# Who issues the reload of the residual: the sync engine among its weight slots, or ScalarE ahead of its casts

## What is computed

```
x   = x   + gate   * (concat(branches, latent)  @ w_out[l])
ctx = ctx + gate_c * (concat(branches, context) @ w_out[l])    # layers 0 and 2 only
```

## Time and profile before

| | us |
|---|---|
| median of 3 runs (3209.92 to 3211.33) | 3210.18 |
| the profiled execution | 3207.1 |
| its span | 3205.3 |
| TensorE busy in it | 3001.5 (94%) |
| VectorE, ScalarE busy | 1604.0, 1023.6 |
| mean granted TensorE clock | 0.969 of full |

### The profile page before, as it was taken

One profiled execution on the slowest core, in us unless ns is written; L12 is line 12 of the kernel. 1 busy time (PEld: TensorE's weight loads), 2 busy tenths in 40 slices (PEclk: granted clock), 3 DMA queues, 4 the chain that ended last, 5 costly groups with the idle time before them and its releaser, 6 DMA issues. The chain is left out here.

```text
span 3205.3 us, 40895 instructions
## 1 busy us (share of the span) xinstructions
PE 3001.5 (94%) x17158; PEld 2356.6 (74%) x17158; DVE 1604.0 (50%) x2493; ACT 1023.6 (32%) x1508; POOL 102.1 (3%) x157
## 2 busy tenths in 40 slices
PE   5899999999997999998969999999989979999988
PEld 1577777786775787886847779667767758797888
DVE  2334343356435553455555472555564355738574
ACT  2212233224212333433323221334442123215453
POOL 0000000000000000000000000430000000003100
PEclk7899999999998999999989999999999989999999
DMA  7644433321544544632844444323345533222455
GB/s 322 280 161 148 145 119 130 113 79 47 208 169 166 213 165 147 248 125 79 310 173 152 157 158 158 131 99 133 135 175 188 183 101 118 82 90 93 145 166 170
DMA packets 120135, 495.10 MB, mean 154 GB/s; under 512 B 11792, under 2 KB 30480, under 8 KB 95120
## 3 DMA queue, kind: packets, MB, share of 16 engines
q1 hardware_dynamic: 99648, 463.51, 40.6%
q10 hardware_dynamic: 20304, 28.97, 2.6%
HBM read 484.05 MB, written 8.39 MB: 154 GB/s over the span
## 5 line engine op out<-in xcount | busy, mean ns | idle before, releaser
L1307 PE MATMUL products<-h_high,w_high 128*128 128x512 f32 (+1 forms) x3424 | 1256.4, 367 | 89.3 <-DVE h_low L936 45.7
L1307 PE MATMUL products<-h_low,w_high 128*128 128x512 f32 (+1 forms) x3424 | 1189.6, 347 | 0.0
L1307 PE MATMUL products<-h_high,w_low 128*128 128x512 f32 (+1 forms) x3424 | 1189.3, 347 | 0.0
L853 DVE TENSOR_TENSOR w_low<-w_raw,w_high 128x1024 fp32r<-128x1024 f32 x500 | 615.3, 1231 | 817.8 <-ACT w_high L550 815.0
L550 ACT CAST w_high<-w_raw 128x1024 fp32r<-128x1024 f32 x500 | 522.8, 1046 | 1381.0 <-PE products L1307 1332.0
L1307 PEld LDWEIGHTS products<-h_high,w_high 128*128 128x128 f32 x3424 | 658.0, 192 | 340.1 <-issue 226.9
L1307 PEld LDWEIGHTS products<-h_low,w_high 128*128 128x128 f32 x3424 | 659.6, 193 | 81.0 <-issue 13.0
L1307 PEld LDWEIGHTS products<-h_high,w_low 128*128 128x128 f32 x3424 | 657.9, 192 | 81.6
L1307 PE MATMUL products<-w_high,h_high 128*128 128x256 f32 x640 | 184.1, 288 | 0.5 <-issue 0.5
L1307 PE MATMUL products<-w_high,h_low 128*128 128x256 f32 x640 | 181.1, 283 | 0.0
L1307 PE MATMUL products<-w_low,h_high 128*128 128x256 f32 x640 | 181.0, 283 | 0.0
(11 more groups left out here) (193 smaller groups left out, 2639.9 us busy)
## 6 DMA issues: line engine op xcount, KB each, us to landing
w_raw<-w_slots SPq DMA_DIRECT2D x500, 512.0 KB, 3.5
ada_w<-ada_slots SPq DMA_DIRECT2D x174, 1024.0 KB, 6.0
mix_b<-ada_slots SPq DMA_DIRECT2D x18, 1024.0 KB, 9.7
x_residual<-x ACTq DMA_DIRECT2D x2, 4096.0 KB, 23.1
x_scratch<-x_residual ACTq DMA_DIRECT2D x3, 2048.0 KB, 7.9
x_residual<-x_scratch ACTq DMA_DIRECT2D x3, 2048.0 KB, 9.2
x_residual<-ctx ACTq DMA_DIRECT2D x2, 2048.0 KB, 15.0
out<-x_residual ACTq DMA_DIRECT2D x1, 2048.0 KB, 7.8
```

What stands on the lines that cost most here:

```text
L853: nc.vector.tensor_tensor(wlo[:, n % SPL, :], raw[:, n % RAW, :], whi[:, n % SPL, :].bitcast(F32), ALU.subtract).then_inc(low_done, 1)
L1307: ins = nc.tensor.matmul(o, a, b, start=first and q == 0, stop=last and q == 2, skip_group_check=skip)
```

## The change

The reloads leave ScalarE's `ysplit`. SP issues them in the first round of `out`, ahead of s4, and waits for the ends of the phases before `ysplit` first.

```diff
+            def x_again(pi):
+
+                layer = PH[pi - 1]["layer"]
+                for s in ends.values():
+                    sp.wait_ge(s, pi - 1)
+                if layer == 0:
+                    sp.dma_start(xT[:, :, :], dram["x0"]).then_inc(x_in, 16)
+                    return
+
+                sp.wait_ge(x_out, 16 * layer)
+                sp.dma_start(xT[:, :, LAT], dram["x_scratch"]).then_inc(x_in, 16)
+                if layer < 3:
+
+                    sp.dma_start(xT[:, :, 0:S], dram["ctx2"]).then_inc(x_in, 16)
...
                         for k in range(8):
+                            if ph["name"] == "out" and i == 0 and k == 4:
+                                x_again(pi)
                             slot(n0 + 8 * i + k)
...
                     layer = ph["layer"]
-                    if layer == 0:
-                        act.dma_start(xT[:, :, :], dram["x0"]).then_inc(x_in, 16)
-                    else:
-                        act.wait_ge(x_out, 16 * layer)
-                        act.dma_start(xT[:, :, LAT], dram["x_scratch"]).then_inc(x_in, 16)
-                        if layer < 3:
-
-                            act.dma_start(xT[:, :, 0:S], dram["ctx2"]).then_inc(x_in, 16)
```

More of the change, by code:

```diff
@@ L456, in unit @@
                 sp.dma_start(place, was[u, :, :]).then_inc(landed, 16)
-            for ph in PH:
+            def x_again(pi):
[9 more added lines that the diff above has]
+                    sp.dma_start(xT[:, :, 0:S], dram["ctx2"]).then_inc(x_in, 16)
+            for pi, ph in enumerate(PH):
                 at = ph["at"]
```

## The result

| | before | after |
|---|---|---|
| median of 13 runs (us) | 3210.18 (3206.49 to 3211.90) | 3217.85 (3214.25 to 3221.73) |
| ratio | | 1.0027, 95% interval 1.0019 to 1.0034 |
| the profile's span | 3205.3 | 3214.0 |
| TensorE busy | 3001.5 (94%) | 3003.5 (93%) |

The change costs 7.7 us. The forecast was 9.7 us and slower.

A forecast was written before the change was run, and what follows sets the result against it. TensorE was taken as busy nearly throughout, with the reload's issues on its path at hand-overs. 6.8 - 0.1 + 0.6 - 0.5 + 2.2 + 1.7 - 1.0 = +9.7 us on 3210.2 gave 3219.9, range 3209 to 3234.

The forecast's parts named there:

- The gain: Hand-overs of all four layers: ScalarE's reload issues leave the path, removing 7.9 us.
- The place of the loss: First round of out: s4's weights land behind a unit and the reload in SP's queue, after 5.77 MB.
- The transfer term: SP's queue, from the unit's issue to s4's landing: 19.6 us, between 18.3 and 25.1.
- Layer 1: s4 starts 6.8 us later, clock +2.2 after an 11 us wait, -1.0 from the shorter hand-over.
- the hand-over's clock: Layer 1: hand-over wait shrinks from 5.12 to 1.65 us, restart costs 1.7 instead of 2.75 us, -1.0.
- Layer 2: s4 starts at -0.1 us, the 3.49 gained given back; TensorE stands 3.4 us, clock +1.7.
- the row at 2.45: Profile row: after 2.45 us of waiting the clock averaged 0.77; used for the +1.7 us before layer 2's s4.
- Layer 0: s4 starts 0.6 us later, TensorE standing 1.0 us before it, with no clock cost.
- Layer 3: Reload goes out at the hand-over, s4 only after s0, so the issue gain is kept: -0.5 us.
- Only the issues go: Rival: SP's queue holds nothing back, no new wait arises, only 7.9 us of issues go; 3202.3 us, chance 0.07.
- The reload is just covered: Rival: SP's queue keeps 402 GB/s, s4 lands in 16.3 us, layer 2 without wait; 3210.8 us, chance 0.20.
- The queue backs up: Rival: SP is held until the reload drains, transfers fall toward end-to-end, +20 to +30; 3235 us, chance 0.10.

The follow-up runs named there:

- late_wait: The change, with VectorE's wait for the reload moved from the entry of out to its first addition to x; 3217.12 us, ratio to before 1.0023.
- act_late_late_wait: The kernel before, with the reload issued by ScalarE behind the cast of s2 and VectorE's wait at the first addition to x; 3211.5 us, ratio 1.0005.
- only_l1: The change in layer 1 alone, the other layers reloading from ScalarE at the head of ysplit; 3215.49 us, ratio to before 1.0016.
- before_late_wait: The kernel before, with nothing but VectorE's wait for x moved to the first addition; 3208.17 us, ratio 1.0000.
- act_first: The kernel before, with ScalarE issuing table, then reload, behind its first four chunks and the cast of s1, VectorE waiting at the first addition; 3202.77 us, ratio 0.9976.
- sp_early: The change, with SP issuing the reload right behind s3, ahead of the unit, at the hand-over itself; 3207.7 us, ratio to before 0.9993.
- but_l1: The change in layers 0, 2 and 3, layer 1 reloading from ScalarE at the head of ysplit; 3210.3 us, ratio to before 1.0007.
- act_late: The kernel before, with the reload issued by ScalarE in its own queue behind the cast of s2, VectorE waiting on entry to out; 3233.36 us, ratio 1.0078.
- act_late_rope: As act_late, but layer 1's rotary table load issued ahead of the reload instead of behind it; 3235.09 us, ratio to before 1.0076.
- act_late_rope_wait: As act_late_rope, with VectorE's wait for x at the first addition; 3216.3 us, ratio to before 1.0019.
- act_first_entry: As act_first, but with VectorE's wait for x at the entry of out; 3212.2 us, ratio to before 1.0009.

## Why the prediction was right

**The gain**, 7.9 us of issue time on the path: right. Waits on the first chunk were forecast at 12.4 us and are 12.2.

**The place of the loss**, the weights of s4 behind a unit and the reload in one queue: right, and shown by s4's landing 1.3 us behind the reload, by late_wait (no change with VectorE's wait moved) and by layer 2 of act_late_late_wait (no wait at all with the reload in another queue).

**The transfer term**, 19.6 us from the unit to the landing of s4: right. To the cast 19.5 in layer 1 and 18.35 in layer 2; in layer 0 16.3 for a forecast of 17.2.

**Layer 1**, +6.8 +2.2 -1.0 = +8.0: measured +6.3 in the profile of the change, +5.7 in only_l1's. The term mis-sized is the hand-over's clock. I left the restart after 1.65 us a cost of 1.7 by the nearest row; it ran at 1.00. s0 was done sooner and the whole chain with it: SP's unit went out 5.3 us after the hand-over, where the forecast had 7.7. The 11 us of standing (11.03) and the 2.2 of clock behind it (2.3) came as written.

**Layer 2**, -0.1 +1.7: measured -1.1. TensorE stood 2.10 us instead of 3.4, and was granted 1.00 behind it. About 1 us of the difference is the transfer, 18.35 us instead of 19.6. The rest is the step that failed, the one that took a wait near 2.45 us to be like the row at 2.45. That row was one outcome of two: the same 2.45 us at the same place were followed by a mean of 0.77 in before and only_l1, and by 1.00 in before_late_wait. The +1.7 rested on a single profile.

**Layer 0**, +0.6: no gap before s4, so its small gain is kept, by a few tenths (183.7 us against 183.9 in before_late_wait, neither with a low stretch at s0). **Layer 3**, -0.5: as forecast where the clock is alike (90.8 against 90.3 in act_first and 90.4 in sp_early).

So the steps that I could place sum to about +4 to +5 (6.3, -1.1, about -0.4, -0.5), where the forecast had +9.7; and the runs say +7.7. The forecast total was nearer than its parts, and that is luck: it had 1.7 us too much in layer 1, 2.7 in layer 2 and about 1 in layer 0, and left out some 3 us that lie elsewhere. but_l1, which ought to gain 2 by the same steps and loses 1 to 2, says the same. The last section names a candidate for 1.8 of them.

**The rivals.** *Only the issues go*: false, 11 us of new wait. *The reload is just covered*: false for layer 1; in layer 2 nearly so (18.35 us with a 2.10 us wait, where it took 16.2 to be hidden). *The queue backs up*: its premise is right and its price wrong. SP was held, 4.26 us in the second reload and 6.49 in the issue of s4 (5.85 in layer 2), so s5 went out only at 1534.1. But s5 landed 1.3 us behind s4, so the transfers followed each other closely and never fell toward the end-to-end bound. s5 to s7 brought no further wait: the lateness at s6 (6.2 us) is that at s31 (6.3).

## What to carry to other kernels

Before moving a transfer off an engine that stands in front of its casts, write down what it will stand ahead of in the new queue, and when it starts: the 7.9 us of issue were gained, and a start 6.1 us later, ahead of the next weights, cost more. Here a big transfer with a late consumer did best in a queue without urgent ones behind it, early, a few instructions behind the critical ones of the engine that issues it, with its consumer waiting where the data is used and not on entering the phase. Neither the early issue behind the first casts nor the late wait was worth anything alone; together they gave 7.3 us. And where two waits cover each other, as the table's issue and the wait for `x` in act_late, removing the one that ends first changes nothing.

## What the runs showed of the hardware

- **An issue can stand for many microseconds behind large transfers.** The third DMA instruction behind two reloads of 2 MB in 1 KB pieces took 16.02 us to issue on ScalarE in act_late and 16.14 in act_late_late_wait. On SP in the change the second reload took 4.26 and the slot behind it 6.49. Behind `x0`, 4 MB in pieces of 32 KB, SP's next slot took 1.45. I expected a queue with room.
- **A queue of its own doesn't make a transfer sooner.** In layer 1 the context's half landed 16.8 us after issue in SP's queue ahead of the weights, and 25.1 us (act_late_rope) and 35.6 us (act_late_rope_wait) in ScalarE's queue beside them, the longer where TensorE, and so SP, went on. The Trainium skill (DMA: Bandwidth & Descriptors, "Issuing engines are not separate DMA queues") says that DMAs of all issuers run on the same 16 engines and interleave. The runs agree, but its corollary, that a second issuer saves issue time only, falls short here: which queue decided who of the two was late, the weights (cast at 24.8 us) or `x` (weights at 15.6, `x` 15 us behind them).
- **The length of a short wait didn't decide the clock.** TensorE waited 2.04 us before s4 of layer 1 in act_first and 2.10 us before s4 of layer 2 in the change. It had been busy throughout ahead of both. Then it was granted 0.53 for 3.5 us in the first and 1.00 in the second (first two rows of act_first, then two of the change):

```profile
1522.00:1530.00 8.00, 8.00 (x65) 6.12 (x64) 3.19 (x7) 2.66 (x6) 0.00 (x0) 1.00 1.06 398
1532.04:1535.50 3.46, 3.46 (x17) 3.46 (x18) 1.23 (x1) 0.31 (x1) 0.00 (x0) 0.53 1.01 389
```

```profile
2425.00:2434.00 9.00, 9.00 (x43) 7.10 (x45) 1.47 (x3) 0.00 (x0) 0.00 (x0) 1.00 1.09 360
2436.86:2446.10 9.24, 9.23 (x40) 7.62 (x41) 2.34 (x2) 1.05 (x1) 0.00 (x0) 1.00 0.62 231
```

At the hand-over of layer 0 the wait of 2.07 or 2.08 us was followed by a mean of 0.77 over 7.5 us in three kernels (act_late_late_wait, act_first_entry, but_l1) and by 1.00 in the seven others that have it.

- **One wait, two clocks.** In `mix` of layer 3, code that no kernel here touches, TensorE waits 3.4 us for GpSimd. Before the change the following matmuls ran at 1.00, after it at 0.50 for 5.9 us, and the code between s31 of layer 2 and the hand-over of layer 3 took 516.4 us instead of 513.6 (line, TensorE; the two rows are of before and of after in this order):

```profile
2988.78 1.99 PE L1648 MATMUL products<-mix_a,w_raw 128*128 128x256 f32 x8 [3.37 <-POOL mix_a L530]
```

```profile
2996.48 3.78 PE L1657 MATMUL products<-mix_a,w_raw 128*128 128x256 f32 x8 [3.36 <-POOL mix_a L547]
```

The same low stretch is in the profiles of all five kernels in which TensorE stood before s4 of layer 2 (the change, late_wait, but_l1, act_late, act_late_rope), and in one of the eight others (act_late_rope_wait). The low stretch at the hand-over of layer 3 is shorter by half where it is there, which gives back about 1 us. That leaves 1.8 of the microseconds missing above. With one profile for each kernel I can't say that it is in every run, nor what ties it to layer 2, and tried nothing that would; that stays open.
